# A transformer block on one Trainium2 core: the latent attention's queries are normed from a single mean, its opening runs in another tile order, and its head outputs are rounded straight from PSUM

## What is computed

```
def _rmsnorm(x, g):
    y = x32 * lax.rsqrt(jnp.mean(x32 * x32, axis=-1, keepdims=True) + EPS)
    return y * g
...
h = _rmsnorm(x, g[1])
c_q = _rmsnorm(h @ w_dq, q_norm)                      # 1024 -> 512
q = (c_q @ w_uq).reshape(bsz, seq, 16, 128 + 64)      # 16 heads
q_nope, q_rope = jnp.split(q, [128], axis=-1)
q_rope = _rope(q_rope, positions)
s = (q_nope . k_nope + q_rope . k_rope) * 192 ** -0.5, causal
o = softmax(s) @ v
x = x + o.reshape(bsz, seq, 2048) @ w_out
```

## Time and profile before

| | us |
|---|---|
| median of 3 runs | 1878.69 |
| lowest, highest | 1873.72, 1879.76 |
| the profiled execution, its own time | 1876.79 |
| its span (first to last instruction) | 1875.0 |
| PE busy | 1796.4 (96% of the span) |
| DVE, ACT, POOL busy | 1212.7, 960.3, 356.2 |
| chain that ended last, by engine | PE 79%, DVE 11%, ACT 5%, issue 3%, DMA 1% |

### The profile page before, as it was taken

How to read it: one execution, slowest core, us unless ns; L and a number is a source line. 1 busy time by engine, 2 the same in 40 slices (tenths; PEclk the granted TensorE clock), 3 DMA queues, 4 the chain that set the end, 5 groups by cost and what they waited for, 6 DMA issues and landing times.

```text
span 1875.0 us, 36715 instructions
## 1 busy us (share of the span) xinstructions
PE 1796.4 (96%) x14496; PEld 1765.3 (94%) x14496; DVE 1212.7 (65%) x1764; ACT 960.3 (51%) x1091; POOL 356.2 (19%) x280
## 2 busy tenths in 40 slices
PE   7999999989999999997998999989899999999999
PEld 7999999979999899996998999988799999989998
DVE  6555689975555665555666655565487776567776
ACT  5444677674444744443333534475365555555453
POOL 2000400020005500034565000366500011020001
PEclk9999999999999999998999999999899999999999
DMA  5556323335554455533343455443344553344452
GB/s 214 217 184 232 125 102 112 131 109 195 185 187 163 152 183 187 190 123 108 118 126 132 180 179 182 181 142 132 127 156 166 182 188 138 128 160 179 179 199 92
DMA packets 45169, 298.25 MB, mean 159 GB/s; under 512 B 5025, under 2 KB 5409, under 8 KB 15921
## 3 DMA queue, kind: packets, MB, share of 16 engines
q1 hardware_dynamic: 45104, 297.38, 44.6%
HBM read 296.31 MB, written 1.05 MB: 159 GB/s over the span
## 4 chain that ended last, share of the span: by engine, by line
PE 79%; DVE 11%; ACT 5%; issue 3%; DMA 1%; POOL 0%; SPq 0%; ACTq 0%; DVEq 0%
PE wk L371 15%; PE wk L373 15%; PE wk L372 15%; PE acc L371 9%; PE acc L373 8%; PE acc L372 8%; DVE x_lo L448 2%; DVE sumsq L669 1%; PE wk L382 1%; PE wk L381 1%; PE wk L383 1%; PE wk L1023 1%; DVE x L413 1%; ACT w_hi L317 1%; ACT tmp L610 1%
## 5 line engine op out<-in xcount | busy, mean ns | idle before, releaser
L317 ACT ACTIVATE w_hi<-raw 128x2048 fp32r<-128x2048 f32 (+5 forms) x300 | 532.5, 1783 | 433.7 <-PE wk L373 361.7
L372 PE MATMUL wk<-x_lo,w_hi 128*128 128x256 f32 x2560 | 726.0, 284 | 0.0
L371 PE MATMUL wk<-x_hi,w_hi 128*128 128x256 f32 x2208 | 631.6, 286 | 16.6 <-DVE x_lo L448 13.0
L2532 POOL TENSOR_TENSOR w_lo<-raw,w_hi 128x512 fp32r<-128x512 f32 (+1 forms) x274 | 355.5, 1331 | 1503.8 <-ACT w_hi L317 1503.8
L373 PE MATMUL wk<-x_hi,w_lo 128*128 128x256 f32 x2208 | 626.4, 284 | 0.0
L343 DVE TENSOR_TENSOR w_lo<-raw,w_hi 128x2048 fp32r<-128x2048 f32 (+2 forms) x218 | 484.1, 2222 | 169.6 <-ACT w_hi L317 169.6
L372 PEld LDWEIGHTS wk<-x_lo,w_hi 128*128 128x128 f32 x2560 | 491.8, 192 | 0.6
L371 PEld LDWEIGHTS wk<-x_hi,w_hi 128*128 128x128 f32 x2208 | 425.2, 193 | 20.0 <-DVE x_lo L448 14.4
L373 PEld LDWEIGHTS wk<-x_hi,w_lo 128*128 128x128 f32 x2208 | 424.9, 192 | 0.0
L371 PE MATMUL acc<-h_hi,w_hi 128*128 128x256 f32 x1376 | 393.4, 286 | 18.6 <-DVE h_lo L2121 4.8
L372 PE MATMUL acc<-h_lo,w_hi 128*128 128x256 f32 x1376 | 388.7, 283 | 0.0
(11 more groups left out here) (312 smaller groups left out, 2184.4 us busy)
## 6 DMA issues: line engine op xcount, KB each, us to landing
raw<-w_ffn_loop SPq DMA_DIRECT2D x120, 1024.0 KB, 4.8
raw<-w_conv_loop SPq DMA_DIRECT2D x60, 1024.0 KB, 4.8
raw<-w_mla_loop SPq DMA_DIRECT2D x18, 768.0 KB, 4.2
raw<-w_hgrn_loop SPq DMA_DIRECT2D x10, 896.0 KB, 4.5
raw<-w_ple_gate SPq DMA_DIRECT2D x8, 1024.0 KB, 4.8
raw<-w_odd_loop SPq DMA_DIRECT2D x10, 768.0 KB, 4.2
raw<-w_even_loop SPq DMA_DIRECT2D x6, 1024.0 KB, 4.8
raw<-w_odd_proj SPq DMA_DIRECT2D x6, 1024.0 KB, 4.8
```

Of the source, the lines that this page charges most:

```text
L317: nc.scalar.activation(w_hi[slot][:, 0:n], raw[slot][:, 0:n], ACT.Copy).then_inc(S("hi_ready"), 1)
L371: nc.tensor.matmul(dst, hi, a_hi, start=start, stop=False, skip_group_check=True)
L372: nc.tensor.matmul(dst, hi, a_lo, start=False, stop=False, skip_group_check=True)
L2532: last = nc.gpsimd.tensor_tensor(w_lo[slot][:, a:b], raw[slot][:, a:b], w_hi[slot][:, a:b].bitcast(F32), ALU.subtract)
```

## The change

- The order of the 32 `dq` tiles: for input tiles 0 to 3 all four outputs, then for input tiles 4 to 7 outputs 0 and 1, and last outputs 2 and 3. So bank 0 is complete 8 tiles before bank 1.
- One mean instead of two. With u the unnormed projection, the two norms together are u / sqrt(mean(u^2) + eps * mean(x^2) + eps^2). ACT squares x scaled by sqrt(eps), squares u straight from PSUM in two halves, PE sums all of it in one group in `acc` bank 0, and there is one Ln and one Exp. The scaling of the latents by rstd falls away. The keys of pair 0 no longer wait for a mean.
- The latents are normed, rounded and split tile by tile, normed straight from PSUM, and pair 0's projection takes its tiles in the order in which they come.
- `scores` runs its four nope products first, and waits for `qr` only behind them.
- The multiplication by cos reads PSUM and comes ahead of the copy of the transposed weights; the one by sin writes back to PSUM.
- ACT rounds a pair's output from PSUM in two halves, and DVE takes the rest from PSUM; `h_val` and its copy are gone. The next projection into bank 0 waits for `lo1` instead of for the copy.
- The rounding of the first unit of `proj1` moves behind the latents on ACT, and one rounding at the end of `mla` moves behind the last `hi`.

```diff
+DQ_ORDER = ((range(4), range(4)), (range(4, KD), range(2)), (range(4, KD), range(2, 4)))
...
+    def mla_opening(p):
+        t = mla_proj(p)
+        return [t[n] for n in (0, 4, 1, 5, 16, 17, 18, 2, 19, 3, 6, 7)]
...
-            add(name, 1, 3, 11, lambda i: [("b_w_dq", k, n * P) for k in range(KD) for n in range(4)])
+            add(name, 1, 3, 11, lambda i: [("b_w_dq", k, n * P) for ks, ns in DQ_ORDER for k in ks for n in ns])
...
-                  (2, 10), (3, 12), (1, 16), lambda p: mla_proj(p)[8:16] + mla_proj(p)[:8] + mla_proj(p)[16:])
+                  (2, 10), (3, 12), (1, 16), lambda p: mla_proj(p)[8:16] + mla_opening(p))
...
-            nc.scalar.activation(tmp[:, :, :], x[:, :, :], ACT.Square).then_inc(S("squares"), 1)
+            nc.scalar.activation(tmp[:, :, :], x[:, :, :], ACT.Square, scale=EPS ** 0.5 if name == "dq" else 1.0).then_inc(S("squares"), 1)
...
+        def pe_dq(pe):
+            seg = segs["dq"]
+            outs = [x_tiles(wk[:, n // 2, n % 2 * SEQ:n % 2 * SEQ + SEQ], n % 2 == 0) for n in range(4)]
+            hs = [outs[n][k] for ks, ns in DQ_ORDER for k in ks for n in ns]
+
+            def squares_mean(half):
+                DQ_A.after(pe, 0, f"square{half}")
+                for k in (2 * half, 2 * half + 1):
+                    last = nc.tensor.matmul(dq_mean, const("mean512"), la_sq[:, k * SEQ:k * SEQ + SEQ], start=False, stop=(k == 3),
+                                            skip_group_check=True)
+                return last
+            pe_after_ple(pe, "dq")
+            at = 0
+            for k in range(4):
+                x_lo_ready(pe, "dq", k)
+                use_tiles(pe, seg, 0, at, hs[at:at + 4])
+                at += 4
+            for k in range(4, KD):
+                x_lo_ready(pe, "dq", k)
+                use_tiles(pe, seg, 0, at, hs[at:at + 2], "dq_half", 23)
+                at += 2
+            use_tiles(pe, seg, 0, at, hs[at:])
+            pe.wait_ge(S("sumsq"), norm_index["dq"] + 1)
+            nc.tensor.matmul(dq_mean, const("mean1024"), sumsq[:, :], start=True, stop=False, skip_group_check=True)
+            squares_mean(0)
+            pe_mla_keys(pe, 0, 0, stop=2)
+            squares_mean(1).then_inc(S("mean"), 1)
+            pe_mla_keys(pe, 0, 2)
...
+        def act_dq(act):
+            seg, nn = segs["dq"], norm_index["dq"]
+
+            def square(half):
+                DQ_A.done(nc.scalar.activation(la_sq[:, 512 * half:512 * half + 512], wk[:, half, :], ACT.Square), f"square{half}")
+            act_norm(act, "dq")
+            round_next(act, seg, 0, 0)
+            nc.scalar.activation(dq_eps, eps[:, :], ACT.Square).then_inc(S("dq_eps_ready"), 1)
+            round_next(act, seg, 0, 1)
+            act.wait_ge(S("dq_half"), 1)
+            square(0)
+            nc.scalar.preload_act_table_set(LN_SET)
+            unit_done(act, seg, 0, 2)
+            square(1)
+            act.wait_ge(S("dq_eps_ready"), 1)
+            act.wait_ge(S("mean"), nn + 1)
+            nc.scalar.activation(la_ln, dq_mean, ACT.Ln, bias=dq_eps).then_inc(S("ln_mean"), 2)
+            act.wait_ge(S("ln_mean"), 2 * nn + 2)
+            nc.scalar.activation(la_rms, la_ln, ACT.Exp, scale=-0.5).then_inc(S("rstd_ready"), 2)
+            for k in range(4):
+                DQ_V.after(act, 0, f"normed{k}")
+                DQ_A.done(nc.scalar.activation(q_hi[:, k, :], la_n[:, k * SEQ:k * SEQ + SEQ], ACT.Copy), f"hi{k}")
+            round_next(act, seg, 0, 2)
...
+        def dve_dq(v):
+            nc.vector.memset(ml_qr, 0.0).then_inc(S("qr_zeroed"), 1)
+            dve_mla_keys(v, 0)
+            v.wait_ge(S("rstd_ready"), 2 * norm_index["dq"] + 2)
+
+            def normed(k):
+                u = wk[:, k // 2, k % 2 * SEQ:k % 2 * SEQ + SEQ]
+                DQ_V.done(nc.vector.scalar_tensor_tensor(la_n[:, k * SEQ:k * SEQ + SEQ], u, param("b_q_norm", k), la_rms, ALU.mult, ALU.mult),
+                          f"normed{k}")
+
+            def lo(k):
+                DQ_A.after(v, 0, f"hi{k}")
+                DQ_V.done(nc.vector.tensor_tensor(q_lo[:, k, :], la_n[:, k * SEQ:k * SEQ + SEQ], q_hi[:, k, :].bitcast(F32), ALU.subtract),
+                          f"lo{k}")
+            normed(0)
+            normed(1)
+            for k in range(2):
+                lo(k)
+                normed(k + 2)
+            lo(2)
+            lo(3)
...
+            use_tiles(pe, *proj_place("mla", i), at + first, hs[first:stop])
+            if stop == 8:
+                vs = [token_tile(lambda b: wk[:, 3, b * SEQ:b * SEQ + SEQ], c_hi[:, k, :], c_lo[:, k, :], k == 0) for k in range(2)]
+                use_tiles(pe, *proj_place("mla", i), at + 4, vs, "mla_kv_done", at + 7, wide=2)
...
+            def project_opening():
+                seg, at = proj_place("mla", 0), 8
+                for k in range(2):
+                    DQ_V.after(pe, 0, f"lo{k}")
+                    use_tiles(pe, *seg, at, [q_tiles[0][k], q_tiles[1][k]])
+                    at += 2
+                DQ_V.after(pe, 0, "normed3")
+                use_tiles(pe, *seg, at, rope_tiles[:2])
+                at += 2
+                for k in range(2, 4):
+                    DQ_V.after(pe, 0, f"lo{k}")
+                    use_tiles(pe, *seg, at, [rope_tiles[k], q_tiles[0][k]], "mla_projected", 16)
+                    at += 2
+                use_tiles(pe, *seg, at, q_tiles[1][2:])
...
+                ML_V_OUT.after(pe, i - 2, "lo1")
+                use_tiles(pe, *seg, 0, q_tiles[0] + q_tiles[1], "mla_q_done", 7)
+                ML_V_SOFT.after(pe, i - 1, "masked")
+                pe_mla_keys(pe, i, 0)
+                use_tiles(pe, *seg, 16, rope_tiles, "mla_projected", 19)
...
 
+                ML_V_NOPE.after(pe, i, "qn")
+                ML_V_KEYS.after(pe, i, "v_tmp")
+                ML_V_PT.after(pe, i - 1, "pt")
+                parts = [(h, c, n, slice(h * SEQ + b * P, h * SEQ + b * P + P)) for h in range(2) for b, (c, n) in enumerate(((0, P), (P, SEQ)))]
+                for h, c, n, q in parts:
+                    nc.tensor.matmul(wk[:, 2 + h, c:c + n], ml_qn[:, q], ml_kn[:, h * SEQ:h * SEQ + n],
+                                     start=(c == 0), stop=False, skip_group_check=True)
                 ML_V_ROT.after(pe, i, "qr")
-                ML_V_PROJ.after(pe, i, "v_tmp")
-                ML_V_PT.after(pe, i - 1, "pt")
-                for h in range(2):
-                    for b, (c, n) in enumerate(((0, P), (P, SEQ))):
-                        q = slice(h * SEQ + b * P, h * SEQ + b * P + P)
-                        nc.tensor.matmul(wk[:, 2 + h, c:c + n], ml_qn[:, q], ml_kn[:, h * SEQ:h * SEQ + n],
-                                         start=(b == 0), stop=False, skip_group_check=True)
-                        last = nc.tensor.matmul(wk[:, 2 + h, c:c + n], ml_qr[:, q], k_rope[:, 0:n], start=False, stop=True,
-                                                skip_group_check=True)
+                for h, c, n, q in parts:
+                    last = nc.tensor.matmul(wk[:, 2 + h, c:c + n], ml_qr[:, q], k_rope[:, 0:n], start=False, stop=True,
+                                            skip_group_check=True)
                 ML_P_SCORES.done(last, "scores")
...
-            project(0)
+            pe.wait_ge(S("ln_mean"), 2 * norm_index["dq"] + 2)
             pe_clear_acc(pe, "mla")
+            project_opening()
...
-            ML_V_OUT.after(pe, B_PAIRS - 1, "lo")
+            ML_V_OUT.after(pe, B_PAIRS - 1, "lo0")
             use_tiles(pe, out1, 0, 0, out_tiles(2)[:KD])
+            ML_V_OUT.after(pe, B_PAIRS - 1, "lo1")
...
             def hi(i):
-                ML_V_OUT.after(act, i, "o")
+                ML_P_O.after(act, i, "o")
                 need(act, "unit_used", out_used("mla", i))
-                ML_A_OUT.done(nc.scalar.activation(h_hi[:, :, :], h_val[:, :, :], ACT.Copy), "hi")
+                for k in range(2):
+                    ML_A_OUT.done(nc.scalar.activation(h_hi[:, k, :], wk[:, 0, k * SEQ:k * SEQ + SEQ], ACT.Copy), f"hi{k}")
...
+            hi(B_PAIRS - 1)
             round_next(act, out0, 0, 0)
-            hi(B_PAIRS - 1)
...
+            def rope(i):
+                if type(i) is int and i == 1:
+                    unit_done(v, *proj_place("mla", 1), 1)
+                else:
+                    v.wait_ge(S("mla_projected"), 1 if type(i) is int and i == 0 else i)
+                nc.vector.scalar_tensor_tensor(ml_qa, wk[:, 1, 0:SEQ], B_SCALE, cos[:, :], ALU.mult, ALU.mult)
+                ML_V_ROPE.done(nc.vector.tensor_scalar(ml_qr0, wk[:, 1, 0:SEQ], B_SCALE, None, ALU.mult), "qr0")
...
-                mul(ml_qa, ml_qr0, cos[:, :])
                 ML_P_ROT.after(v, i, "rot")
-                ML_V_ROT.done(mul(ml_qb, wk[:, 1, SEQ:512], sin[:, :]), "turned")
+                turned = wk[:, 1, SEQ:512]
+                ML_V_ROT.done(mul(turned, turned, sin[:, :]), "turned")
                 ML_V_ROT.after(v, i, "turned")
```

(16 more changed lines are left out.)

222 lines of the change are left out of this document (90 added, 132 removed).

## The result

| | before | changed |
|---|---|---|
| median, us | 1877.12 (4 runs, 1873.72 to 1879.76) | 1854.76 (4 runs, 1853.12 to 1859.32) |
| profiled execution, its own time | 1876.79 | 1859.32 |
| its span | 1875.0 | 1857.5 |
| chain that ended last, PE and DVE | 79%, 11% | 81%, 10% |

The ratio is 0.9895, with a 95% interval of 0.9874 to 0.9917: 1.05% faster. The prediction said 1855.0, in a range of 1849 to 1862.

What follows compares the result with a forecast made beforehand. PE, busy 96% of the span, bounds the kernel, so gains come only from its waits and half clock. Terms sum to 23.0 us: 1876.8 becomes 1853.8, plus 1.9 for the median 1855.7, stated as 1855, range 1849 to 1862.

Steps and rivals of the forecast that it cites:

- opening, to the first tile behind `scores(0)`: From the end of the 32 `dq` tiles: shorter waits and full clock bring that tile from 876.0 to 861.45, gaining 14.5 us.
- pair 1: `scores(1)` no longer waits 2.02 us for the turned part nor runs at half clock (about 1.75): gain 3.75 us.
- loop, `transpose(1)` to `transpose(6)`: PE's 0.43 us wait for values goes, about 0.25 for rotation comes: 0.2 a pair, 0.65 us in all.
- wait for `h_lo` ahead of `out0`: At the attention's end, PE's wait of 1.22 us for `h_lo` becomes 0.1: gain 1.15 us.
- ahead of `out1`: Behind `o(7)`, 3.11 us of copy, rounding and rest become 1.45, two roundings and one half rest: gain 1.65 us.
- clock at the end: 28 slower matmuls at the attention's end gain 2.6 us if PE stays at full clock; half was taken, 1.3.
- the copies: In the opening, DVE's copies of keys and values end behind Exp and are on the path by 1.2 us.
- The wait of 1.9: Opening: PE waits 1.9 us for the first `q_lo` at full clock; rival, half clock, 1857 to 1860, chance 0.20.
- Table load: Rival in the opening: a load holds ACT 1.4 us longer, `lo0` 0.2 to 1.4 later; 1856, chance 0.04.
- Weights: First `proj1` unit ready at 860.1, used at 861.45; rival: `project(1)` starts up to 3 us late, 1858, chance 0.05.
- wait for `lo1`: Rival in the loop: bank 0, held until `lo1`, costs each pair 0.3 to 0.7 us; 1857 to 1860, chance 0.10.

Runs made afterwards that it cites:

- `scores_old`: The changed kernel with nope and rope score products in turn again, all behind the wait for `qr`: 1855.86 us, 0.9892 of the kernel before.
- `via_hval`: The changed kernel with each pair's output copied to `h_val` in SBUF again, rounded and split from there in halves: 1865.09 us, 0.9947 of the kernel before.
- `whole_sbuf`: The changed kernel with the output copied to SBUF, one rounding and one rest from there, as before the change: 1857.59 us, 0.9903 of the kernel before.
- `whole_psum`: The changed kernel with one rounding and one rest of the output from PSUM instead of two halves: 1854.54 us, 0.9882 of the kernel before.
- `change_again`: The changed kernel itself, unaltered, run once more to look at PE's clock: 1859.37 us.

## Why the prediction was right

| step, as predicted | us | measured |
|---|---|---|
| opening, to the first tile behind `scores(0)` | 14.5 | 14.44 |
| pair 1 (with it, to `transpose(1)`: 18.25) | 3.75 | 4.14 (18.58) |
| loop, `transpose(1)` to `transpose(6)` | 0.65 | 0.71 |
| wait for `h_lo` ahead of `out0` | 1.15 | 0.67 |
| ahead of `out1` | 1.65 | 1.85 |
| clock at the end | 1.3 | 1.55 |
| sum | 23.0 | 23.36 |

- **The opening** went as worked out, and for those reasons. `lo0` was forecast 7.87 us behind the first mean (853.4) and let PE go on at 7.84; the projection's end 12.4, measured 12.27; the nope scores 13.3, measured 13.22; the next projection 15.9, measured 15.75. Inside, one error stayed hidden. Ln to the end of Exp took 2.55 instead of 2.20, and Exp ended 5.70 behind the mean instead of 5.27; but norming waits for DVE's copies, which are bound to PE's values and not to Exp, and it began at 6.40, where 6.47 was forecast. So the copies are on the path by 0.68, not by 1.2, and a change that only takes them away gains no more than that.
- **The wait of 1.9** was 1.75 and the clock stayed up, as I chose. That it did so in this execution is in part luck: in two of the six with this wait it fell. The chance of one in five for that is not at odds with two in six.
- **Table load.** The rival fell: removing the load gave back its 1.28 and nothing else.
- **Weights.** The first unit was rounded at 860.62 (9.3 behind the mean; forecast 9.6) and `project(1)` did not wait.
- **Pair 1.** The size was right. Of its two reasons, nope products first and shorter adds, only the second was needed: sin, cos and the adds from PSUM (`scores_old`); the nope products ahead of the wait bring their 1.3 in pair 0 alone.
- **The loop.** PE's 0.43 for the values went and about 0.22 for the scaled rope part came (forecast 0.25). No wait for `lo1` showed in any pair; PE came to the bank 0.7 us behind the second rest, where the forecast had 0.2 to 0.3. The rests from PSUM took 0.42 each beside POOL, as I took from L1811. On this the page "SBUF — State Buffer" of the Trainium skill, section "Who interferes with whom", says that a DVE instruction with two SBUF inputs contends with a GpSimd one that reads SBUF, and that one with at most one SBUF input does not, unless it runs in a 2-port mode, which a copy can enter. The runs agree: L1904 takes 0.42 on average in the loop, L1909 of `via_hval` 1.50. The prediction left the exception out. What I had not priced is the copy of the values (L1911), SBUF to SBUF: it took 1.07 on average in the loop before and 0.45 now, since it starts ahead of POOL's instruction and not within it (within one, in pair 1, it still takes 1.35).
- **The end.** The 1.22 for `h_lo` went (1.22 less 0.1 is 1.12, the sum has 1.15), but 0.43 came for the softmax, which I had not named: what is late next behind a wait removed. The 1.65 ahead of `out1` was right in size and too simple in cause. I put all of the shorter rest to PSUM. `whole_sbuf` waits 2.24 there, with its rest at 0.69 since POOL is idle: of the 1.90 us from 3.11 to 1.21, 0.87 come from the rounding of `out0`'s next unit that now stands behind `hi(7)` and keeps POOL away, and 1.03 from the change of path, 0.82 by PSUM and 0.21 by the halves (`whole_psum` waits 1.42). The wait left was forecast at 1.4 to 1.5 and is 1.21. The clock stayed up and gave more than the half of 2.6 that I took, but 0.88 came back as a wait ahead of `ffn3`; where the clock fell (`change_again`), 1.5 were lost.
- **The whole.** 1854.76 lies on 1855 partly by luck: the profiled execution, against which the sum was made, took 1859.32 where the sum says 1853.8, for a stretch of lower clock 600 us ahead of the change.

## What to carry to other kernels

A wait in front of a full matrix engine can cost more than its length: here 14.5 us of waits took 8.8 us of lower clock with them, and either half of the change alone saved 2 us of slow matmuls in the opening where both saved 6.3. So waits that stand close together are worth removing together. A subtraction of a rounded part should read its source from PSUM when GpSimd works beside it, and where it must read SBUF, it should be one wide instruction and not two halves, since each is held for what is left of GpSimd's instruction. When a few us matter, count from a point just ahead of the change: the whole time moved by up to 8 us for reasons that lay elsewhere.

## What the runs showed of the hardware

- A vector subtraction or addition with both operands in SBUF that started within an instruction of POOL ended 0.28 us (256 columns) or 0.55 us (512) behind the end of that instruction, whenever it had started. In the loop this made about 1.05 us per instruction, whatever its width (one of 512 columns 1.75 instead of 0.69, two of 256 2.92 instead of 0.76); with one operand in PSUM it paid nothing.
- A vector copy from SBUF to SBUF of 512 columns took 0.43 when it started before POOL's instruction, and 0.56 to 1.42 when it started within it, by how much of it was left; it ended 0.28 us behind the end of POOL's. I had looked only at instructions with two operands.
- The clock behind one and the same wait differed between executions: behind 1.75 us it fell to half in two of six, behind 2.72 us in its one execution it did not, behind 3.78 us it did.
- The stretch 230 to 260 us, which the change does not touch, was granted 0.94 in six of the thirteen profiled executions, 0.83 in two and 0.74 to 0.77 in five. The first mean of `dq` came at 845.5 to 847.1 us in the first, at 848 in the second and at 851.3 to 853.5 in the third. What sets this stayed open.
